# Depthwise convolution of a decoder step: 25 of 31 taps of two channel chunks on TensorE instead of one

## What is computed

```python
    hm = _rmsnorm(x, g_mix) * (1 + scm) + shm
    proj = hm @ w_in
    a = proj[..., :D_CONV]
    g = proj[..., D_CONV:2 * D_CONV]
    u_pool = proj[..., 2 * D_CONV:]
    u_conv = a * jax.nn.sigmoid(g)
    conv_ext = jnp.concatenate([conv_prev, u_conv], axis=1)
    v = _depthwise_causal_conv(conv_ext, w_dw, b_dw)
    v = jax.nn.silu(_layernorm(v, ln_g, ln_b))
    ...
    mix = jnp.concatenate([v, p], axis=-1) @ w_out
    x = x + gtm * mix
```

## Time and profile before

| | |
|---|---|
| median of 3 runs | 1164.72 us (1164.26 to 1165.55) |
| span of the profiled execution | 1163.8 us |
| PE busy | 1102.1 us, 95% |
| DVE busy | 380.0 us, 33% |
| ACT busy | 317.3 us, 27% |
| POOL busy | 422.3 us, 36% |

### The profile page before, as it was taken

The page is one execution under the profiler, slowest core; times in us unless marked ns, Lnnn a source line. Parts: engine busy times, 40 slices in busy tenths (PEclk is TensorE's granted clock), DMA queues, the critical chain, the costliest instruction groups (busy, mean ns, idle before and its releaser), DMA issues.

```text
span 1163.8 us, 19733 instructions
## 1 busy us (share of the span) xinstructions
PE 1102.1 (95%) x8278; PEld 1057.4 (91%) x8278; DVE 380.0 (33%) x665; ACT 317.3 (27%) x358; POOL 422.3 (36%) x164
## 2 busy tenths in 40 slices
PE   8899999999999999994949799999999999999996
PEld 7799999999999999794945597999999999999996
DVE  3611111111111115689999634411111111211144
ACT  4522211222211223442224324432211222112232
POOL 2233333243332434356463032343333333433432
PEclk8999999999999999897979998999999999999998
DMA  8744222243222352242126412222222222222222
GB/s 325 288 161 181 75 107 72 98 157 112 104 73 73 109 192 98 109 182 73 37 70 177 145 51 95 74 73 78 102 73 73 92 88 72 80 101 73 72 73 81
DMA packets 21651, 127.00 MB, mean 109 GB/s; under 512 B 4192, under 2 KB 5344, under 8 KB 7008
## 3 DMA queue, kind: packets, MB, share of 16 engines
q1 hardware_dynamic: 15456, 96.06, 23.4%
q10 hardware_dynamic: 6144, 30.19, 7.3%
HBM read 123.06 MB, written 3.19 MB: 108 GB/s over the span
## 4 chain that ended last, share of the span: by engine, by line
PE 45%; issue 38%; POOL 7%; DVE 7%; DVEq 1%; ACT 1%; POOLq 0%; ACTq 0%
PE tile_a L352 20%; PE tile_b L352 20%; POOL w_lo L1118 6%; DVE v L1055 2%; PE ada_ps L333 2%; DVE v L1052 1%; PE tile_a L441 1%; DVE sq L937 1%; DVE sq L940 1%; PE stat_ps L398 1%; PE stat_ps L406 0%; DVEq L1055 0%; DVE hm_lo L924 0%; ACT hm_hi L631 0%; POOL w_lo L1127 0%
## 5 line engine op out<-in xcount | busy, mean ns | idle before, releaser
L1118 POOL TENSOR_TENSOR w_lo<-w_raw,w_hi 128x2048 fp32r<-128x2048 f32 x75 | 346.6, 4622 | 622.5 <-ACT w_hi L599 622.5
L352 PE MATMUL tile_b<-hm_hi,w_hi 128*128 128x288 f32 x864 | 188.2, 300 | 23.4 <-DVE conv_s L1026 23.4
L352 PE MATMUL tile_a<-hm_hi,w_hi 128*128 128x288 f32 x864 | 189.0, 301 | 13.7 <-DVE hm_lo L924 9.5
L599 ACT ACTIVATE w_hi<-w_raw 128x2048 fp32r<-128x2048 f32 x78 | 148.7, 1906 | 175.6 <-PE tile_b L352 175.5
L352 PE MATMUL tile_b<-hm_lo,w_hi 128*128 128x288 f32 x864 | 188.2, 300 | 0.0
L352 PE MATMUL tile_b<-hm_hi,w_lo 128*128 128x288 f32 x864 | 187.8, 299 | 0.0
L352 PE MATMUL tile_a<-hm_lo,w_hi 128*128 128x288 f32 x864 | 185.7, 297 | 0.0
L352 PE MATMUL tile_a<-hm_hi,w_lo 128*128 128x288 f32 x864 | 185.7, 297 | 0.0
L958 DVE TENSOR_TENSOR full<-sil,tile_b 128x576 f32<-128x576 f32 x44 | 33.2, 754 | 458.1 <-PE tile_b L352 458.1
L352 PEld LDWEIGHTS tile_b<-hm_hi,w_hi 128*128 128x128 f32 x864 | 141.8, 192 | 23.9 <-DVE conv_s L1026 23.9
L352 PEld LDWEIGHTS tile_a<-hm_hi,w_hi 128*128 128x128 f32 x864 | 139.4, 190 | 24.2 <-issue 12.1
(11 more groups left out here) (146 smaller groups left out, 1138.0 us busy)
## 6 DMA issues: line engine op xcount, KB each, us to landing
w_raw<-w_units SPq DMA_DIRECT2D x78, 1024.0 KB, 4.9
ada_raw<-w_ada ACTq DMA_DIRECT2D x28, 1024.0 KB, 6.6
ada_raw<-w_ada SPq DMA_DIRECT2D x8, 1024.0 KB, 5.5
x<-x_in SPq DMA_DIRECT2D x4, 576.0 KB, 6.1
y_out<-x SPq DMA_DIRECT2D x8, 288.0 KB, 2.4
conv_s<-conv_state SPq DMA_DIRECT2D x1, 480.0 KB, 7.6
conv_s_out<-conv_s ACTq DMA_DIRECT2D x1, 480.0 KB, 7.4
wp_raw<-w_pool SPq DMA_DIRECT2D x1, 256.0 KB, 8.4
```

The costliest lines, as they stand in the source:

```text
L352: mm = pe.matmul(ps[:, h, 0:HALF], w[:, w_slot, cols], r[:, k, HALF * h:HALF * (h + 1)], start=(first and n == 0), stop=(last and n == 2))
L599: nc.scalar.activation(w_hi[:, side, :], w_raw[:, side, :], ACT.Copy).then_inc(w_hi_ready, 1)
L1118: nc.gpsimd.tensor_tensor(w_lo[:, side, :], w_raw[:, side, :], w_hi[:, side, :].bitcast(F32), ALU.subtract).then_inc(w_lo_ready, 1)
```

## The change

A second chunk is treated like the last one. `PE_CHUNKS` is chunks 2 and 3. `conv_batch` now counts ten batches: 0 to 4 are chunk 2, accumulated in `tile_b`, 5 to 9 are chunk 3, in `tile_a`. The new batches follow batch 4 directly in PE's stream, and their diagonals stand in ACT's stream behind `pmix_round(3)`. DVE keeps six taps of chunk 2 and adds both PSUM tiles at the end. `ln_sum(2)` waits for the first pair of additions, `ln_sum(3)` for the second.

```diff
@@ -75,7 +75,9 @@
 TAP_GROUPS = (WIDTH - 1) // TAPS_PER_LOOP
 PE_BATCHES = 5
 PE_TAP0 = WIDTH - PE_BATCHES * TAPS_PER_LOOP
-DVE_TAPS = (CONV_CHUNKS - 1) * WIDTH + PE_TAP0
+PE_CHUNKS = (CONV_CHUNKS - 2, CONV_CHUNKS - 1)
+FIRST_TAP = (0, WIDTH, 2 * WIDTH, 2 * WIDTH + PE_TAP0)
+DVE_TAPS = FIRST_TAP[-1] + PE_TAP0
 
 Y_POOL = (KD - 2, KD - 1)
 
@@ -501,26 +503,26 @@
 
             def conv_batch(b):
 
-                c = CONV_CHUNKS - 1
+                c, ps = PE_CHUNKS[b // PE_BATCHES], tiles[1 - b // PE_BATCHES]
                 if b == 0:
                     pe.wait_ge(tile_read[1], OUT)
                     pe.wait_ge(tile_read[0], OUT)
                 for kk in range(TAPS_PER_LOOP):
-                    k = PE_TAP0 + b * TAPS_PER_LOOP + kk
+                    k = PE_TAP0 + b % PE_BATCHES * TAPS_PER_LOOP + kk
                     pe.wait_ge(diag_ready, b * TAPS_PER_LOOP + kk + 1)
-                    pe.matmul(tile_a[:, 0, 0:SEQ], diag[:, kk, :], conv_p[:, c, k:k + SEQ],
+                    pe.matmul(ps[:, 0, 0:SEQ], diag[:, kk, :], conv_p[:, c, k:k + SEQ],
                               start=(k == PE_TAP0), stop=(k == WIDTH - 1))
-                    mm = pe.matmul(tile_a[:, 1, 0:DEC_BATCH * DEC_SEQ], diag[:, kk, :],
+                    mm = pe.matmul(ps[:, 1, 0:DEC_BATCH * DEC_SEQ], diag[:, kk, :],
                                    conv_s[:, c, DEC_BATCH * k:DEC_BATCH * (k + DEC_SEQ)],
                                    start=(k == PE_TAP0), stop=(k == WIDTH - 1))
                     mm.then_inc(diag_used, 1)
 
             def ln_sum(c):
 
-                if c < CONV_CHUNKS - 1:
+                if c not in PE_CHUNKS:
                     pe.wait_ge(conv_tap, 2 * WIDTH * (c + 1))
                 else:
-                    pe.wait_ge(pe_taps_added, 2)
+                    pe.wait_ge(pe_taps_added, 2 * (c - PE_CHUNKS[0] + 1))
                 for h in range(2):
                     mm = pe.matmul(stat_ps[:, h, 0:HALF], ones[:], v[:, c, HALF * h:HALF * (h + 1)],
                                    start=(c == 0), stop=(c == CONV_CHUNKS - 1))
@@ -536,7 +538,8 @@
             conv_batch(3)
             ada_turn(6)
             pool_product(3)
-            conv_batch(4)
+            for b in range(4, 2 * PE_BATCHES):
+                conv_batch(b)
             pe.wait_ge(pmix_full, GROUPS)
             for c in range(CONV_CHUNKS - 1):
                 ln_sum(c)
@@ -768,7 +771,7 @@
                 for kk in range(TAPS_PER_LOOP):
                     if b:
                         act.wait_ge(diag_used, (b - 1) * TAPS_PER_LOOP + kk + 1)
-                    w = V_WDW + (CONV_CHUNKS - 1) * WIDTH + PE_TAP0 + b * TAPS_PER_LOOP + kk
+                    w = V_WDW + PE_CHUNKS[b // PE_BATCHES] * WIDTH + PE_TAP0 + b % PE_BATCHES * TAPS_PER_LOOP + kk
                     nc.scalar.activation(diag[:, kk, :], ident[:], ACT.Copy, scale=col(w)).then_inc(diag_ready, 1)
 
             glu_gate(0)
@@ -813,6 +816,8 @@
             pmix_round(2)
             pmix_read(3)
             pmix_round(3)
+            for b in range(5, 2 * PE_BATCHES):
+                diagonals(b)
             for a in range(ADA_QUARTERS * 8 - 1, ADA_QUARTERS * 8 + 1):
                 ada_load(a)
 
@@ -1046,7 +1051,7 @@
                 with dve.Fori(g0, g1) as g:
                     for kk in range(TAPS_PER_LOOP):
                         k = g * TAPS_PER_LOOP + (kk + 1)
-                        done = g * (2 * TAPS_PER_LOOP) + 2 * (kk + 1 + c * WIDTH)
+                        done = g * (2 * TAPS_PER_LOOP) + 2 * (kk + 1 + FIRST_TAP[c])
                         win_p, win_s, w = window(c, k)
                         dve.wait_ge(conv_tap, done - 1)
                         nc.vector.scalar_tensor_tensor(prompt(vc), win_p, w, prompt(vc), ALU.mult,
@@ -1067,17 +1072,18 @@
             conv_taps(1, TAP_GROUPS - 2, TAP_GROUPS)
             glu(3)
             conv_start(2)
-            conv_taps(2, 0, TAP_GROUPS)
+            conv_taps(2, 0, TAP_GROUPS - PE_BATCHES)
             mod_evacuate(6)
             conv_start(3)
             conv_taps(3, 0, TAP_GROUPS - PE_BATCHES)
 
-            dve.wait_ge(diag_used, WIDTH - PE_TAP0)
             dve.wait_ge(conv_tap, 2 * DVE_TAPS)
-            vc = by_half(v[:, CONV_CHUNKS - 1, :])
-            nc.vector.tensor_tensor(prompt(vc), prompt(vc), split2(tile_a[:, 0, 0:SEQ]), ALU.add).then_inc(pe_taps_added, 1)
-            nc.vector.tensor_tensor(sample(vc), sample(vc), split2(tile_a[:, 1, 0:DEC_BATCH * DEC_SEQ]),
-                                    ALU.add).then_inc(pe_taps_added, 1)
+            for n, c in enumerate(PE_CHUNKS):
+                dve.wait_ge(diag_used, (n + 1) * (WIDTH - PE_TAP0))
+                vc, ps = by_half(v[:, c, :]), tiles[1 - n]
+                nc.vector.tensor_tensor(prompt(vc), prompt(vc), split2(ps[:, 0, 0:SEQ]), ALU.add).then_inc(pe_taps_added, 1)
+                nc.vector.tensor_tensor(sample(vc), sample(vc), split2(ps[:, 1, 0:DEC_BATCH * DEC_SEQ]),
+                                        ALU.add).then_inc(pe_taps_added, 1)
 
             dve.wait_ge(ln_sum_done, 1)
             for c in range(CONV_CHUNKS):
```

## The result

| | median, us | runs |
|---|---|---|
| before | 1164.79 | 1164.26 to 1165.55 |
| changed | 1186.59 | 1185.14 to 1188.12 |

The ratio is 1.0186, with a 95% interval of 1.0171 to 1.0200: 21.8 us slower. The forecast was 22.5 us slower, 1187.2 us with a range of 1184.5 to 1189.6.

A forecast was written before the change was run, and what follows sets the result against it. PE was taken as the bound, with DVE ending last before the layer norm and costing PE only 4.5 us idle. 27.0 us of added taps minus 4.5 gave +22.5 us on 1164.7: 1187.2 us, range 1184.5 to 1189.6.

The forecast's parts named there:

- The added taps: On PE, behind batch 4 and ahead of the first channel sum: 25 taps at 1.08 us, 27.0 us, all on the path.
- cheaper taps: Rival: in an unbroken row on PE the small matmul hides wholly, 0.92 us a tap, +18.5 us, 1183.2 us; chance 0.05.
- the half level: Rival: PE's clock falls to half during the new taps; if all 25, +46.0 us, 1210.7 us; chance 0.07 for part or all.
- The split of a tap into 0.92 and 0.16 us: On PE: 0.92 us from a tap's large matmul to its small one, 0.16 us more to the next tap.
- The idle time given back: PE's waits behind its taps, 1.36 us for DVE's chunk 2 taps and 3.12 us for its additions, vanish: -4.5 us.
- The wait at `mod_evacuate(6)`: DVE, done with its six chunk 2 taps, waits some 21 us for PE's `ada_turn(6)`; costs nothing.
- The diagonals: 25 more on ACT at 0.40 us each, hidden behind PE's taps of 1.08 us; cost nothing.
- The transfers of pieces 31 and 32: On ACT's queue behind batch 9's diagonals: first landed at about 680, its product starts at 684.7, some 5 us left.
- The dip: Clock falls to half level at 660 to 664 in the layer norm's small matmuls, losing 1.7 us; change taken as zero, bounds ±1.7.
- the dip goes: Rival: with PE's idle time ahead removed, the clock fall at 660 disappears; 1185.5 us; chance 0.22.
- Around the span: The runs' median was taken to lie 0.9 us above the profiled span: 1186.3 us span, 1187.2 us forecast.
- Not slower: Rival: `glu` comes earlier, added taps fill PE's 15.5 and 7.3 us idle stretches; zero or below, down to 1164.4; chance 0.02.

The follow-up runs named there:

- the row of 5, 15 and 25 taps: Changed kernel with PE taking 5, 15 or 25 (the change itself) of chunk 2's taps: 1165.91, 1177.02 and 1186.59 us.
- the five-tap kernel: Changed kernel with PE taking 5 instead of 25 taps of chunk 2: 1165.91 us, ratio 1.0009 to the kernel before.
- first experiment: Changed kernel with DVE's `mod_evacuate(6)` moved behind its taps of chunk 3: 1186.59 us, ratio 1.0184 to the kernel before.
- the `glu` placed anew and 25 taps: Changed kernel with `glu(1)` after 3 and `glu(2)` after 5 groups of chunk 0, `glu(3)` right after `conv_start(1)`: 1150.16 us, ratio 0.9863 to the kernel before.

## Why the prediction was right

**The added taps.** 25 x 1.08 = 27.0 was forecast, 27.04 measured, at clock 1.00. That they all lie on the path is shown by the row of 5, 15 and 25 taps, and by the 4.9 us that came back when their small matmuls went. The rivals of cheaper taps and of the half level did not come. The split of a tap into 0.92 and 0.16 us was wrong (0.86 and 0.22), but the sum used only the whole. The 28.5 us at clock 1.00 held against the half level are not taps alone: about 3 us of them are conditioning and pooling products.

**The idle time given back.** 4.5 us, as forecast: both waits are gone. In the five-tap kernel 5.4 us of taps lengthen the stretch by 0.8 us (by 0.6 counted from the fourth tap, 39.45 against 38.86), so 4.6 to 4.8 us came back.

**What was costed at nothing.** The wait at `mod_evacuate(6)` was 22.1 us, forecast some 21, and costs nothing (first experiment). Behind it DVE needed 643.67 - 635.85 = 7.8 us up to chunk 2's additions, and not 5.5: two small rows took 1.4 us each, beside POOL work. That too had time to spare. The diagonals cost nothing (no difference without them). The transfers of pieces 31 and 32, from ACT's timeline, which answers to the earlier trace rows:

```profile
673.03 1.20 ACTq L587 DMA_DIRECT2D ada_raw<-w_ada  x2
```

Forecast were 672.9 for them and 684.7 for their product. It starts at 683.76 with no idle time ahead of it.

**The dip.** I took zero, with 1.7 us either way in the range. In the profiled execution of the change it is gone. It shows in five small matmuls that follow the one-column sums of the earlier trace rows; from PE's timelines, the kernel before and then the change:

```profile
660.88 1.35 PE L406 MATMUL stat_ps<-ident,rms 128*128 128x128 f32 x5
```
```profile
683.03 0.80 PE L408 MATMUL stat_ps<-ident,rms 128*128 128x128 f32 x5
```

Here the term was off for this execution, and it is the 1.4 us by which the rest of the span got shorter. But the kernel without new diagonals, with the same PE stream, has 1.35 us in this row again and 511.6 behind the centring. So the dip comes and goes from one execution to another, and nothing shows the rival "the dip goes" to be a property of the change. Of the 13 profiled executions, four have 0.80 us in this row and 509.9 to 510.4 behind the centring; the other nine have 1.04 to 1.35 in it and 511.3 to 512.3 behind. So one execution can be 1.4 us faster or slower than another with nothing changed. The rival's cause, the idle time ahead, also falls: with 5 taps PE has no idle time ahead of the sums and the row still takes 1.35, and with the `glu` placed anew and 25 taps PE was busy for 131.82 us without a gap and the granted clock still fell to 0.50 at 643 us. The median's 21.8 us lie between 22.2 (the stretch alone) and 21.1 (the stretch and the dip).

**Around the span.** 0.9 us was mis-sized. The profiled execution of the change took 1186.73 us with a span of 1184.9, so 1.8 lie around it. I had set the span of one execution of the kernel before against the median of others. In the profiled execution, a span 1.4 us shorter than the forecast 1186.3 and 0.9 more around it nearly cancel, which is luck. The difference of the medians does not contain this term: 22.5 against 21.8.

**"Not slower".** It did not come, for the reason given: every moved tap stood behind `glu(3)`. As a mechanism it was right. It wanted the `glu` to come earlier; once they do, 1186.6 becomes 1150.2. The 1164.4 that I worked out for it was too high. It let the added taps fill two idle stretches and gave nothing for the third (23.3 is the sum of 15.5 and 7.9) and for the half level behind the idle time.

## What to carry to other kernels

Moving work off an engine pays only from the point where that engine ends last, and at most what the other engine waits there: find that idle time in the timeline before counting the work. If the waits that matter lie ahead of the removed work in a fixed instruction order, the order has to change with the split; each change alone lost or gave almost nothing, and together they gave 1.4%. A small matmul can have a price floor that its columns do not tell (here 0.22 us from 32 to 128 columns), so cost it by taking it out and not by the distance between two starts.

## What the runs showed of the hardware

In a row of taps at granted clock 1.00, an fp32 matmul of 64 columns with 128 x 128 weights cost 0.22 us, and 32 or 128 columns changed that by less than 0.01; one of 512 columns cost 0.86.

The clock fell to its half level behind one-column matmuls in nine profiled executions and not in four. Kernels with the same PE stream stand on both sides, and it fell with and without idle time ahead. It cost 1.4 us or a little more. What decides it stays open.

DVE's tap instructions lasted up to 4.9 us instead of 0.28 or 0.75 while POOL worked, and all 37 long ones of the kernel before stood beside POOL work.
